# Retention mixer: the gate projected token by token, and the gate applied together with the head norm, ahead of the transposes

## Time and profile before

| | us |
|---|---|
| median of 3 runs | 2657.62 |
| lowest, highest | 2657.22, 2663.17 |
| the profiled execution | 2657.14 |
| its span, first to last instruction | 2655.3 |
| PE busy | 2617.9 |
| DVE busy | 1802.4 |
| ACT busy | 1418.5 |
| retention stage in the trace, about | 1770 to 1972 |

### The profile page before, as it was taken

The page is one execution under the profiler, slowest core; times in us unless marked ns, Lnnn a source line. Parts: engine busy times, 40 slices in busy tenths (PEclk is TensorE's granted clock), DMA queues, the critical chain, the costliest instruction groups (busy, mean ns, idle before and its releaser), DMA issues.

```text
span 2655.3 us, 45241 instructions
## 1 busy us (share of the span) xinstructions
PE 2617.9 (99%) x18380; PEld 2330.2 (88%) x18380; DVE 1802.4 (68%) x2201; ACT 1418.5 (53%) x1882; POOL 142.5 (5%) x229
## 2 busy tenths in 40 slices
PE   9999999999999999999999999999999999999999
PEld 8899989788898888889988888889988888889887
DVE  6676788766657666679757666666566676666765
ACT  6555567544555455458435455453445454455544
POOL 4000000100000000001210000000100000000000
PEclk9999999999999999999999999999999999999999
DMA  7187899655545555544215556555456555554553
GB/s 219 45 282 252 276 323 352 210 190 180 175 139 191 190 175 199 190 142 144 98 34 192 190 175 209 190 180 192 139 172 205 190 183 190 190 167 143 185 190 124
DMA packets 366196, 491.82 MB, mean 185 GB/s; under 512 B 12337, under 2 KB 321169, under 8 KB 366033
## 3 DMA queue, kind: packets, MB, share of 16 engines
q1 hardware_dynamic: 363008, 480.37, 54.6%
q0 software_dynamic: 2576, 7.97, 1.0%
q10 hardware_dynamic: 448, 1.12, 0.1%
HBM read 488.38 MB, written 1.05 MB: 184 GB/s over the span
## 4 chain that ended last, share of the span: by engine, by line
PE 91%; DVE 4%; ACT 3%; issue 1%; POOL 1%; DMA 0%; ACTq 0%; DVEq 0%; POOLq 0%
PE bank_all L368 22%; PE bank_all L367 11%; PE bank_all L347 8%; PE bank_all L349 8%; PE bank_all L348 8%; PE acc_all L347 8%; PE acc_all L349 8%; PE acc_all L348 8%; DVE w_lo L2062 1%; PE acc_all L3371 1%; PE bank_all L3379 1%; ACT w_hi L1947 1%; DVE w_lo L317 1%; PE bank_all L1846 0%; PE bank_all L1847 0%
## 5 line engine op out<-in xcount | busy, mean ns | idle before, releaser
L317 DVE TENSOR_TENSOR w_lo<-raw,w_hi 128x2048 fp32r<-128x2048 f32 x348 | 797.2, 2294 | 391.0 <-ACT w_hi L312 390.9
L312 ACT ACTIVATE w_hi<-raw 128x2048 fp32r<-128x2048 f32 x349 | 667.4, 1915 | 279.7 <-PE acc_all L349 222.5
L368 PE MATMUL bank_all<-act_both,w_hi 128*128 128x512 f32 x2560 | 654.8, 392 | 1.5 <-DVE w_lo L317 1.5
L368 PEld LDWEIGHTS bank_all<-act_both,w_hi 128*128 128x128 f32 x2560 | 465.2, 189 | 84.8 <-DVE w_lo L317 2.0
L367 PEld LDWEIGHTS bank_all<-act_both,w_lo 128*128 128x128 f32 x2560 | 349.2, 190 | 25.1
L347 PE MATMUL acc_all<-w_hi,mix_hi 128*128 128x512 f32 x920 | 360.9, 392 | 2.1 <-DVE mix_lo L3887 1.0
L349 PE MATMUL acc_all<-w_hi,mix_lo 128*128 128x512 f32 x920 | 358.5, 390 | 0.0
L348 PE MATMUL acc_all<-w_lo,mix_hi 128*128 128x512 f32 x920 | 358.1, 389 | 0.0
L367 PE MATMUL bank_all<-act_both,w_lo 128*128 128x256 f32 x2560 | 357.0, 282 | 0.0
L992 ACT ACTIVATE scratch<-bank_all 128x256 f32<-128x256 f32 x320 | 122.1, 385 | 426.4 <-PE bank_all L368 420.0
L347 PE MATMUL bank_all<-act_both,w_hi 128*128 128x256 f32 x1016 | 291.1, 286 | 5.7 <-DVEq L2201 2.1
(11 more groups left out here) (602 smaller groups left out, 3729.5 us busy)
## 6 DMA issues: line engine op xcount, KB each, us to landing
raw<-in_ffn_w_gu SPq DMA_DIRECT2D x176, 1024.0 KB, 5.1
raw<-in_ffn_w_down SPq DMA_DIRECT2D x88, 1024.0 KB, 5.0
raw<-in_ml_w_in SPq DMA_DIRECT2D x24, 1024.0 KB, 5.3
raw<-in_rt_w_in SPq DMA_DIRECT2D x24, 1024.0 KB, 5.1
raw<-in_w_up SPq DMA_DIRECT2D x20, 1024.0 KB, 6.5
raw<-in_w_down SPq DMA_DIRECT2D x19, 1024.0 KB, 5.6
raw<-in_w_gate SPq DMA_DIRECT2D x18, 1024.0 KB, 6.9
moe_raw<-in_w_gate SPq DMA_DIRECT2D x14, 1024.0 KB, 7.0
```

The costliest lines, as they stand in the source:

```text
L312: act.activation(w_hi[0:rows, slot, 0:size], raw[0:rows, slot, 0:size], ACT.Copy).then_inc(hi_made, 1)
L317: dve.tensor_tensor(w_lo[0:rows, slot, 0:size], raw[0:rows, slot, 0:size], w_hi[0:rows, slot, 0:size].bitcast(F32), ALU.subtract).then_inc ...
L368: return pe.matmul(bank[b][:, :], w_hi[:, slot, w], act_both[:, k, :], start=k == 0, stop=k == KT - 1)
```

```diff
-        def pe_rows(pe, slot, k0, start, hi=mix_hi, lo=mix_lo):
-            for k in range(2):
-                for t in range(TT):
-                    for half in range(2):
...
+        def pe_rows(pe, slot, k0, start, hi=mix_hi, lo=mix_lo, second_half=None):
+            order = [(k, t) for k in range(2) for t in range(TT)]
+            if second_half:
+                order.sort(key=lambda kt: kt[1])
+            for k, t in order:
+                if second_half and (k, t) == (0, 1):
+                    second_half()
+                for half in range(2):
...
-                pe_rows(pe, (c.p + j) % RING, k0, j == 0, hi, lo).then_inc(tensor_done, 1)
+                pe_rows(pe, (c.p + j) % RING, k0, j == 0, hi, lo, second_half if j == 0 else None).then_inc(tensor_done, 1)
+                if behind and j == 1:
+                    behind()
...
-                if x == "v":
-                    banks = [result("v", j - j % 2 + t) for t in range(TT)]
+                if x in "vg":
+                    banks = [result(x, j - j % 2 + t) for t in range(TT)]
...
             retained(2)
+            project("g", 4)
             turn(1)
-            project("g", 4)
             retained(3)
             project("g", 5)
+            project("g", 6)
             turn(2)
-            project("g", 6)
             project("g", 7)
-            turn(3)
             rt_moved(c)
             def ready(j):
                 if j == 0:
-                    rt_dve.wait(pe, "scaled3")
+                    rt_dve.wait(pe, "scaled2")
                 rt_dve.wait(pe, f"low{j}")
-            pe_out_panels(pe, c, 8, ready, lambda j: rt_out(2 * j))
+            pe_out_panels(pe, c, 8, ready, lambda j: rt_out(2 * j), lambda: rt_dve.wait(pe, "scaled3"), lambda: turn(3))
...
                     act.wait_ge(tensor_done, E[x, j])
-                    last = act.activation(rt_g[:, 2 * j:2 * j + 2, :], pair, ACT.Silu)
-                    last.then_inc(evacuated[N[x, j] % BANKS], 1)
+                    for t in range(TT) if j % 2 else ():
+                        n = N["g", j - 1 + t] % BANKS
+                        act.activation(rt_g[:, t, (j - 1) * PW:(j + 1) * PW], bank[n][:, :], ACT.Silu).then_inc(evacuated[n], 1)
...
                 for t in range(TT):
-                    last = dve.tensor_scalar(scratch[:, t, h % 2 * RT_DV:h % 2 * RT_DV + RT_DV], rt_y(h, t)[:, :],
-                                             rt_rs[:, 2 * h + t:2 * h + t + 1], None, ALU.mult)
+                    wait_evacuated(dve, N["g", 2 * h + t])
+                    last = dve.scalar_tensor_tensor(scratch[:, t, h % 2 * RT_DV:h % 2 * RT_DV + RT_DV], rt_y(h, t)[:, :],
+                                                    rt_rs[:, 2 * h + t:2 * h + t + 1], rt_g[:, t, h * RT_DV:(h + 1) * RT_DV],
+                                                    ALU.mult, ALU.mult)
...
             ahead("g", 1)
             scaled(0)
             ahead("g", 2)
+            low(0)
+            ahead("g", 3)
             scaled(1)
-            mixed(0)
-            ahead("g", 3)
-            scaled(2)
-            low(0)
-            mixed(1)
             ahead("g", 4)
             low(1)
-            scaled(3)
             ahead("g", 5)
-            mixed(2)
+            scaled(2)
             ahead("g", 6)
             ahead("g", 7)
-            mixed(3)
+            scaled(3)
             low(2)
+            rt_moved(c)
+            for j in range(2):
+                dve_ahead(dve, c.p + j)
             low(3)
-            rt_moved(c)
-            for j in range(6):
+            for j in range(2, 6):
                 dve_ahead(dve, c.p + j)
```

More of the change, by code:

```diff
@@ L404, in pe_narrow_turn @@
             return last
-        def pe_rows(pe, slot, k0, start, hi=mix_hi, lo=mix_lo):
-            for k in range(2):
-                for t in range(TT):
-                    for half in range(2):
-                        w, tok = slice(k * D + half * 512, k * D + half * 512 + 512), slice(t * P, t * P + P)
-                        last = split_product(pe, acc[2 * t + half][:, :], hi[:, k0 + k, tok], lo[:, k0 + k, tok],
-                                             w_hi[:, slot, w], w_lo[:, slot, w], start and k == 0, False)
+        def pe_rows(pe, slot, k0, start, hi=mix_hi, lo=mix_lo, second_half=None):
[6 more added lines that the diff above has]
+                for half in range(2):
+                    w, tok = slice(k * D + half * 512, k * D + half * 512 + 512), slice(t * P, t * P + P)
+                    last = split_product(pe, acc[2 * t + half][:, :], hi[:, k0 + k, tok], lo[:, k0 + k, tok],
+                                         w_hi[:, slot, w], w_lo[:, slot, w], start and k == 0, False)
             return last
@@ L2387, in pool_ffn, with pe_out_panels @@
             c.ends("norm", 0.5)
-        def pe_out_panels(pe, c, panels, ready, src):
+        def pe_out_panels(pe, c, panels, ready, src, second_half=None, behind=None):
             for j in range(panels - 2):
@@ L2789, in block_kernel @@
         rt_dve = Steps("rt_dve", ["angle", "swapped"] + [f"rot{j}" for j in range(8)] + [f"S{h}" for h in range(4)]
-                       + ["scaled0", "scaled1", "mixed0", "scaled2", "low0", "low1", "mixed1", "low2", "low3", "scaled3", "mixed2",
-                          "mixed3"] + [f"low{j}" for j in range(4, 8)])
+                       + ["scaled0", "low0", "low1", "scaled1", "low2", "low3", "scaled2", "scaled3"]
+                       + [f"low{j}" for j in range(4, 8)])
         rt_act = Steps("rt_act", ["sin"] + [f"squares{h}" for h in range(4)])
@@ L2796, in block_kernel @@
         RT_EV += [("g", 1), ("y", 0, 0), ("y", 0, 1), ("g", 2), ("y", 1, 0), ("y", 1, 1), ("turn", 0, 0), ("turn", 0, 1)]
-        RT_EV += [("g", 3), ("y", 2, 0), ("y", 2, 1), ("turn", 1, 0), ("turn", 1, 1), ("g", 4), ("y", 3, 0), ("y", 3, 1)]
-        RT_EV += [("g", 5), ("turn", 2, 0), ("turn", 2, 1), ("g", 6), ("g", 7), ("turn", 3, 0), ("turn", 3, 1)]
+        RT_EV += [("g", 3), ("y", 2, 0), ("y", 2, 1), ("g", 4), ("turn", 1, 0), ("turn", 1, 1), ("y", 3, 0), ("y", 3, 1)]
+        RT_EV += [("g", 5), ("g", 6), ("turn", 2, 0), ("turn", 2, 1), ("g", 7)]
+        RT_EV += [("out", 0), ("out", 1), ("turn", 3, 0), ("turn", 3, 1)]
         RT_DONE = {k: j + 1 for j, k in enumerate(RT_EV)}
-        RT_RES = {k: j for j, k in enumerate(k for k in RT_EV if k[0] not in "Sy")}
+        RT_BANKED = [(x, j) for x in "vq" for j in range(8)]
+        for h in (0, 2):
+            RT_BANKED += [("g", 2 * h + j) for j in range(4)] + [("turn", h + j, i) for j in range(2) for i in range(2)]
+        RT_RES = {k: j for j, k in enumerate(RT_BANKED)}
         RT_PAN = {(x, j): 8 * i + j for i, x in enumerate("vqg") for j in range(8)}
@@ L2948, in high @@
             def high(h):
-                rt_dve.wait(act, f"mixed{h}")
                 for i in range(2):
                     hi, lo, k = rt_out(4 * h + 2 * i)
-                    act.activation(hi[:, k:k + 2, :], rt_g[:, 4 * h + 2 * i:4 * h + 2 * i + 2, :],
-                                   ACT.Copy).then_inc(hi_done, 1)
+                    act.wait_ge(tensor_done, E["turn", h, i])
+                    b = bank[N["turn", h, i] % BANKS]
+                    act.activation(hi[:, k:k + 2, :], b[:, :].rearrange("p (m t) -> p m t", m=2), ACT.Copy).then_inc(hi_done, 1)
             for j in range(8):
@@ L2971, in act_rt @@
             squares(2)
+            projected("g", 4)
             high(1)
-            projected("g", 4)
             squares(3)
@@ L3084, in dve_rt @@
             ahead("g", 2)
+            low(0)
+            ahead("g", 3)
             scaled(1)
-            mixed(0)
-            ahead("g", 3)
-            scaled(2)
-            low(0)
-            mixed(1)
             ahead("g", 4)
             low(1)
-            scaled(3)
             ahead("g", 5)
-            mixed(2)
+            scaled(2)
             ahead("g", 6)
             ahead("g", 7)
-            mixed(3)
+            scaled(3)
             low(2)
+            rt_moved(c)
+            for j in range(2):
+                dve_ahead(dve, c.p + j)
             low(3)
-            rt_moved(c)
-            for j in range(6):
+            for j in range(2, 6):
                 dve_ahead(dve, c.p + j)
-            c.p += 8; c.e += 8; c.hi += 8
+            c.p += 8; c.e += 6; c.hi += 8
             c.ends("norm")
```

32 lines of the change are left out of this document (13 added, 19 removed).

## The result

The changed kernel takes 2666.49 us, the median of ten runs (2663.53 to 2669.41). The kernel before, run ten times beside it, takes 2658.51 (2657.22 to 2663.17). The medians are 8.0 us apart. The ratio, 1.0025 with a 95% interval from 1.0017 to 1.0033, says 6.6 us and 4.5 to 8.8. The forecast was 2662.0 with a range up to 2664.7. The difference that it had to its profiled execution, +4.9 us, lies in the interval; its time does not lie in the range. The profiled execution took 2668.58, with a span of 2666.4.

A forecast was written before the change was run, and what follows sets the result against it. PE's queue was taken to bound the stage. From 2657.14 us, -2.5 (panels) + 1.45 + 4.17 (waits) + 0.1 (restart) gave 2660.3, and +1.7 for a clock fall gave 2662.0 us, range 2659.3 to 2664.7.

The forecast's parts named there:

- What bounds the kernel: Whole stage: PE's queue alone bounds it; DVE's and ACT's saved work counts only if it shortens a PE wait.
- Part 1, the gate panels: Eight gate panels go token by token with 24 fewer matmuls each, saving 0.314 us a panel, 2.5 us in all.
- Part 2, the covers: PE's work while scaled is made, against a 6.9 us chain: stalls of 1.45 us at scaled2, 4.17 at scaled3, none elsewhere.
- Part 3, moved and dropped steps at nothing: Moved turn(3), its high and low, the turns' banks, dropped mixed and the out2 panel's split: no cost or gain.
- The sum: Panels and waits together: -2.5 + 1.45 + 4.17 + 0.1 = +3.2 us, giving 2660.3 us.
- Part 4, the clock: Behind the 4.2 us idle time in out0 PE's granted clock likelier than not falls once, costing +1.7 us.
- The third sentence: At turn(2): the 1.45 us stall is shorter than the 2.06 us that cost nothing, so no clock loss, 0.
- The forecast's base and "How the numbers follow": Base: profiled execution, 2657.14 us; range from no fall less 1 us (2659.3) to two falls plus 1 us (2664.7).
- the nearly equal rates of the two forms: Rival on gate panels: the columns' saving is not there, 0.5 at worst 0, time 2664.0 to 2664.5 us; chance 0.04.
- the covered waits: Rival on the waits for scaled: all covered, only the gate panels' saving left, 2654.6 us; chance 0.04.
- the clock that stays low: Rival on the output panels: clock falls at the gap and stays at half, +41 us, 2701; chance 0.04.
- No fall of the clock: Rival behind out0's wait: same stalls, +3.2 us, but the clock stays up, 2660.3 us; chance 0.22.

The follow-up runs named there:

- the version with both first: Changed kernel with scaled2 put ahead of g5's w_lo work and scaled3 ahead of g7's on DVE: stage 183.71 us, ratio to before 0.9991, again 0.9994.

## Why the prediction was wrong, step by step

- **What bounds the kernel**: right. PE's queue bounds the stage, and every us put on it or taken off it counted.
- **Part 1, the gate panels**: right in kind, 10% too large. Eight panels gave 2.26 us (before against the version with both first, which has the new break in out0 too), 0.28 a panel and not 0.314. A panel behind another kind of work takes longer than one in a row of its kind, and a little more so with 512 columns: g3 took 5.58 us after (1897.63 to 1903.21), 5.83 before, 0.13 and 0.07 above the rates of the earlier trace rows. The figure of the Trainium skill for the fixed cost of a matmul ("TensorE: Matmul & The Clock Gate", "Wait — 56ns, not 53.3ns?"), which would have given 0.5 us, is not what this kernel shows.
- **Part 2, the covers**: right. No wait at `scaled0` and `scaled1`; 1.45 and 4.17 us forecast at `scaled2` and `scaled3`, idle 1.25 and 3.91 plus the matmul's overlap. Together 5.7 us, as forecast. Moving `scaled2` and `scaled3` ahead of one w_lo each removed both, so the named cause, the order on DVE, is shown. One reading was off without harm: in the kernel before `scaled3` ran at the end of g5 (DVE at 1916.01, the turn behind g5 at 1916.64), not in its middle.
- **Part 3, moved and dropped steps at nothing**: right; the version with both first has them all and no wait. `low6` has four panels behind the turn (out2 to out5, 22 us) and not three, which only adds to the cover.
- **The sum**: +3.2 forecast for waits and panels, 189.44 - 185.97 = +3.5 measured.
- **Part 4, the clock**: the fall came as taken, at 1.4 us in one execution and 2.3 in another for the 1.7 forecast. The row of 1.7 us was one length of two: the clock stayed low for 3.4 us or for 6.8, a part of it idle. The third sentence, that the shorter wait costs no fall, held. Its ground, that 2.06 us had cost nothing, did not. With the waits' 5.7 us and the panels, that makes +4.9 us in one trace and +5.8 in the other for the +4.9 forecast. The closeness of the first is part luck: the saving was taken 0.25 us too large and the fall 0.3 too dear, and the two cancel.
- **The forecast's base and "How the numbers follow"**: this step failed. The forecast was anchored on one profiled execution at 2657.14, and the text put the 0.5 us between it and the median "within what I can tell". It is the lowest time of all that were shown, and three runs with one at 2663.17 had already said that an execution of this kernel moves by 6 us. Ten runs put the median of before at 2658.51, later sets of 21 and 33 at 2659.38 and 2660.54. The range was made of the case's own mechanisms (no fall, two falls, 1 us for the stalls) and had no term for the spread of executions ahead of the stage. The measured median lies 4.5 us above the forecast. Of that 1.4 is the base, up to 0.9 the longer fall, and at least 2.2 is in no term: it is scatter of the ten executions outside the stage as far as is known, for the next set had the two kernels 5.5 us apart and not 8.0. With a term for it (+1.4 for the median, 2 or more to each side) the range would have held 2666.49.

The rivals: the nearly equal rates of the two forms, the covered waits and the clock that stays low all fell. "No fall of the clock" was seen in none of the four long waits. The prediction set two gaps of about 2.1 us beside the warning of the Trainium skill on long idle gaps ("TensorE: Matmul & The Clock Gate", "Why this matters for your kernels"). The four waits of 3.9 to 4.05 us are the first long ones in this case, and they agree with it.

## What to carry to other kernels

When a step is made to wait for something new, look at what stands ahead of it in its own engine's queue, and put work that is needed 10 us later behind it: here the places of two lines were worth 7 to 8 us of the stage and turned its loss into the gain that the change was for. A cover is counted in what the bounding engine has to do between cause and use, and an idle time of about 4 us on TensorE cost its length plus 1.4 to 2.9 us for the clock here, and one of 2.2 us its length plus 1.5 us or nothing. Make a forecast's range from the spread of the executions too, and don't hang it on a single profiled one, however well the stage is understood.

## What the runs showed of the hardware

- The granted clock stayed at 1.2 GHz for about 3.4 us or about 6.8 us at a time, in the same kernel behind the same idle time (1934.1 to 1937.5 in one execution, 1938.5 to 1945.3 in the other).
- Idle times of 2.05 to 2.3 us were followed by a fall in some executions and by none in others, and so was one of 1.55 us (five of eight traces). The one of 1.25 us in the stage was not followed by one in any of seven traces; those of 3.9 to 4.05 us were all four times.
- The same 3224 PE instructions took 131.2 to 133.9 us in twelve executions without a fall of the clock among them (from PE's wait at 1241 us to that at 1373).
- A plain float32 matmul of 128x512 is two passes of 0.43 us, 3.8 times the 0.227 us of the rounded float32 form.
